# Other places for the third modulation and for the recurrence's steps in a hybrid HGRN2 and attention layer

## The reference

```python
shift_m, scale_m, gate_m, shift_f, scale_f, gate_f = ada_mod(c, w_ada, b_ada)     # silu(c) @ w_ada + b_ada
h = rms_norm(x, gain) * (1 + scale_m) + shift_m
hq, hf, hi, hg, fq, fk, fv, ff = split(h @ w_in)
# recurrence, in blocks of rows: b = cumsum(logf(hf)); k = (1 - lb) * sigmoid(-hf); v = hi
o = (q * exp(b)) @ S + att(q, k, decay of b) @ v
S = exp(b_last) * S + (k * exp(b_last - b)).T @ v
# attention: logf = log_sigmoid(ff + bias); c = cumsum(logf); softmax(q k / 8 + c_q - c_k) v
```

## Time and profile before

| what | us |
|---|---|
| median of 3 runs (773.26 to 776.86) | 774.0 |
| the profiled execution | 773.54 |
| its span, first to last instruction | 771.8 |
| PE busy | 672.2 |
| DVE busy | 381.8 |
| ACT busy | 210.1 |
| POOL busy | 216.3 |

### The profile page before, as it was taken

How to read it: one execution, slowest core, us unless ns; L and a number is a source line. 1 busy time by engine, 2 the same in 40 slices (tenths; PEclk the granted TensorE clock), 3 DMA queues, 4 the chain that set the end, 5 groups by cost and what they waited for, 6 DMA issues and landing times. The chain is left out here.

```text
span 771.8 us, 19078 instructions
## 1 busy us (share of the span) xinstructions
PE 672.2 (87%) x7455; PEld 442.2 (57%) x7455; DVE 381.8 (49%) x1053; ACT 210.1 (27%) x425; POOL 216.3 (28%) x336
## 2 busy tenths in 40 slices
PE   2999999999987969998899992699999999999920
PEld 1686476444443858665764552566666666676710
DVE  3300024200189788666645438455555555555556
ACT  4310137000161132266401110123232222232203
POOL 1212100100397620120100000234444444444440
PEclk9999999999998879999899996699999999999975
DMA  8973082536303110490095129699999999999624
GB/s 334 400 270 109 1 327 89 240 113 256 128 2 113 71 32 2 147 380 21 8 408 230 54 82 368 266 417 414 414 416 416 414 411 411 406 410 410 238 69 183
DMA packets 38417, 182.95 MB, mean 237 GB/s; under 512 B 5912, under 2 KB 6312, under 8 KB 22672
## 3 DMA queue, kind: packets, MB, share of 16 engines
q1 hardware_dynamic: 29968, 158.88, 52.0%
q0 software_dynamic: 8384, 23.12, 8.4%
HBM read 169.57 MB, written 15.28 MB: 240 GB/s over the span
## 5 line engine op out<-in xcount | busy, mean ns | idle before, releaser
L1757 PE MATMUL bank<-weights,x_hT 128*128 128x512 f32 x256 | 113.3, 601 | 0.0
L1741 PE MATMUL bank<-x_hT,weights 128*128 128x272 f32 x384 | 92.5, 403 | 0.0
L2046 PE MATMUL bank<-weights,R 128*32 128x256 f32 x1408 | 80.6, 379 | 5.1 <-issue 4.0
L1741 PEld LDWEIGHTS bank<-x_hT,weights 128*128 128x128 f32 x384 | 74.2, 195 | 16.9 <-issue 0.8
L1757 PEld LDWEIGHTS bank<-weights,x_hT 128*128 128x128 f32 x256 | 48.7, 192 | 60.4 <-issue 60.2
L845 POOL DMA_INDIRECT y_d<-R,x_hT x44 | 50.9, 1156 | 98.0 <-DVE R L1609 46.6
L2046 PEld LDWEIGHTS bank<-weights,R 128*32 128x32 f32 x1408 | 54.2, 110 | 28.5 <-issue 7.3
L1087 ACT ACT_TABLE_LOAD x44 | 56.5, 1283 | 21.0 <-DVEq L1190 20.3
L839 POOL DMA_INDIRECT R<-h_d,x_hT x46 | 48.0, 1044 | 45.8 <-POOL x_hT L858 25.4
L1087 ACT ACTIVATE R<-bank 128x128 f32<-128x128 f32 x44 | 12.2, 278 | 175.9 <-PE bank L2046 175.9
L1975 PE MATMUL bank<-weights,x_hT 128*128 128x512 f32 x128 | 58.3, 608 | 0.0
(11 more groups left out here) (346 smaller groups left out, 994.5 us busy)
## 6 DMA issues: line engine op xcount, KB each, us to landing
weights<-in_w_ada SPq DMA_DIRECT2D x24, 1024.0 KB, 11.1
weights<-in_w_exp_gate SPq DMA_DIRECT2D x16, 1024.0 KB, 10.6
weights<-in_w_exp_down SPq DMA_DIRECT2D x16, 1024.0 KB, 11.3
weights<-in_w_exp_up SPq DMA_DIRECT2D x16, 1024.0 KB, 11.3
R<-in_w_exp_down SPq DMA_DIRECT2D x16, 1024.0 KB, 11.1
weights<-in_w_in SPq DMA_DIRECT2D x7, 2048.0 KB, 8.6
R<-in_w_exp_up SPq DMA_DIRECT2D x8, 1024.0 KB, 10.9
R<-in_w_exp_gate SPq DMA_DIRECT2D x8, 1024.0 KB, 10.9
```

The lines of the kernel that those rows point to most:

```text
L1741: ins = T.matmul(bank[b][:, 0:HALF], w[:, k, h * P:(h + 1) * P], hT[:, k, c * HALF:(c + 1) * HALF], start=(n == 0), stop=(n == KT - 1))
L1757: ins = T.matmul(bank[b][:, :], hT[:, k, i * P:(i + 1) * P], w[:, k, :], start=(k == 0), stop=(k == KT - 1))
L2046: ins = T.matmul(bank[2][32 * j:32 * j + 32, 0:2 * P].rearrange("p (w f) -> p w f", w=2), XT[:, k, :], W2[:, :, k, j * P:(j + 1) * P], sta ...
```

## The change

Four things change, and all of them are order or place; no arithmetic is added or taken away.

1. The modulation's products come earlier: the first half of ada1 ahead of hg, its second half ahead of hf, ada2's halves between hf's heads and ahead of hi. The ring of loads follows. DVE reads ada1 ahead of hf's work and ada2 ahead of hi's copies; POOL stores ada2's rows ahead of all exponents.
2. Tiles of fk, their turns and the gate's logits (ff) move into `schedule`, and the recurrence's steps begin right behind hi: step -1 stands ahead of fk, and the others are spread among fk, ff, fv and fq. lfT stands behind two tiles of fv.
3. fk uses banks 6 and 7 instead of 4 and 5, its turns bank 3 instead of 6.
4. DVE prepares tile 0 of the recurrence between the third and the fourth copy of hi. POOL's stores of fk go between the exponents of tiles 2, 3 and 4, its stores of fv behind them all.

```diff
             grp(f"hg{i}", 2 + i % 2, "act")
+        grp("ada1", 1, "dve")
         for h in range(HGH):
             grp(f"hf{h}0", 4 + 2 * (h % 2), "dve")
             grp(f"hf{h}1", 5 + 2 * (h % 2), "dve")
-        grp("ada1", 1, "dve")
+        grp("ada2", 0, "dve")
         for i in range(NTILE):
             grp(f"hi{i}", 2 + i % 2, "dve")
...
-        schedule = [("fv", i) for i in range(NTILE)] + [("fq", h, c) for h in range(4) for c in range(2)]
-        for step, after in reversed(list(zip(range(-1, NTILE), (1, 4, 6, 8, 10, 11)))):
-            schedule.insert(after + 1, ("hgrn", step))
-        schedule.insert(1, ("lfT",))
+        schedule = [("hgrn", -1), ("fk", 0), ("fk", 1), ("fkT", 0), ("hgrn", 0), ("fk", 2), ("fkT", 1), ("ff",), ("fk", 3), ("fkT", 2),
+                    ("hgrn", 1), ("fk", 4), ("fv", 0), ("fv", 1), ("lfT",), ("fkT", 3), ("fkT", 4), ("hgrn", 2),
+                    ("fv", 2), ("fv", 3), ("fv", 4), ("fq", 0, 0), ("hgrn", 3),
+                    ("fq", 0, 1), ("fq", 1, 0), ("fq", 1, 1), ("fq", 2, 0), ("hgrn", 4), ("fq", 2, 1), ("fq", 3, 0), ("fq", 3, 1)]
...
+            elif item[0] == "fk":
+                grp(f"fk{item[1]}", 6 + item[1] % 2, "act")
+            elif item[0] == "fkT":
+                grp(f"fkT{item[1]}", 3, "dve")
...
-        ring += [("hf", 6, 2), ("hi", 4, 2)] + [(f"ada1_{k}", k - 4, 1) for k in range(4, 8)]
-        ring += [("fk", 6, 2)] + [(f"ada2_{k}", k, 1) for k in range(4)]
-        ring += [("fv", 4, 2)] + [(f"ada2_{k}", k - 4, 1) for k in range(4, 8)]
-        ring += [("fq", 6, 2)]
+        ring += [("hf", 6, 2)] + [(f"ada1_{k}", k - 4, 1) for k in range(4, 8)]
+        ring += [("hi", 4, 2)] + [(f"ada2_{k}", k % 4, 1) for k in range(8)]
+        ring += [("fk", 6, 2), ("fv", 4, 2), ("fq", 6, 2)]
...
-        for r, first in enumerate(("hT00", "hf00", "fk0")):
+        for r, first in enumerate(("hT00", "hg0", "hf20")):
```

On POOL:

```diff
+            mod_rows(2)
...
             exponents(0)
             exponents(1)
             pool.dma_start(S_sample, a["state_hgrn"].rearrange("l b h k v -> k (l b h) v")).then_inc(s_S0, 16)
+            filled(pool, "Db0")
+            exponents(2)
+            store_k(0)
+            store_k(1)
+            filled(pool, "Db1")
+            exponents(3)
+            store_k(2)
+            store_k(3)
+            filled(pool, "Db2")
+            exponents(4)
             taken(pool, "lfT")
...
+            store_k(4)
...
+            filled(pool, "fkT4")
...
+            for i in range(NTILE):
+                store_v(i)
```

On ACT:

```diff
             exp_levels(0)
             exp_ends(0)
             exp_levels(1)
             for item in schedule:
+                if item[0] == "fk":
+                    evict_k(item[1])
+                if item[0] == "ff":
+                    taken(act, "ff1")
+                    alink(act, A.activation(ssel[0:8, 0:TOK], cf[0:8, 0:TOK], ACT.Abs))
```

On DVE:

```diff
+            for i in range(3):
+                evict_v(i)
             dve.wait_ge(s_qs, HGH)
             end_exponents(0)
             operands(0)
             end_operands(0)
+            for i in range(3, NTILE):
+                evict_v(i)
...
             for item in schedule:
+                if item[0] == "fkT":
...
+                if item[0] == "ff":
+                    fox_sums()
```

On PE:

```diff
             feature_major("hq")
+            ada(1, 1, 0, 4)
             loaded(pe, "hg")
             for i in range(NTILE):
                 token_major("hg", i, 2 + i % 2)
-            ada(1, 1, 0, 4)
-            feature_major("hf")
             ada(1, 1, 4, KT)
+            feature_major("hf", range(2))
+            ada(2, 0, 0, 4)
+            feature_major("hf", range(2, 4))
+            ada(2, 0, 4, KT)
             loaded(pe, "hi")
             for i in range(NTILE):
                 token_major("hi", i, 2 + i % 2)
-            ada(2, 0, 0, 4)
-            loaded(pe, "fk")
...
```

More of the change, by code:

```diff
@@ L219, in build @@
                 grp("lfT", 3, "dve")
+            elif item[0] == "ff":
+                grp("ff0", 0, "dve")
+                grp("ff1", 1, "dve")
+                grp("lpT", 2, "dve")
+            elif item[0] == "fk":
+                grp(f"fk{item[1]}", 6 + item[1] % 2, "act")
+            elif item[0] == "fkT":
+                grp(f"fkT{item[1]}", 3, "dve")
             elif item[0] == "fv":
@@ L722, in _, with store_k, store_v @@
             bias_rows(2)
-            for i in range(NTILE):
+            mod_rows(2)
+            def store_k(i):
                 taken(pool, f"fk{i}")
                 pool.dma_start(kout[i * P:(i + 1) * P, :] if i < 4 else kous, fkt[i % 2][0:ROWS[i], :]).then_inc(s_kout[i % 2], 16)
-            mod_rows(2)
+            def store_v(i):
+                taken(pool, f"fv{i}")
+                pool.dma_start(vout[i * P:(i + 1) * P, :] if i < 4 else vous, v_fox[0:ROWS[i], i, :]).then_inc(s_vout, 16)
             def exponents(i):
@@ L737, in exponents @@
                     g.tensor_tensor(Xv[:, :, :, H:], bv[:, :, :, H:], anc, ALU.subtract).then_inc(s_lv, 1)
-            taken(pool, "hi0")
             exponents(0)
@@ L750, in _ @@
             pool.dma_start(cks_d, cf[0:8, SEQ:SEQ + PAST + NDEC]).then_inc(s_ckw, 16)
-            filled(pool, "Db0")
-            exponents(2)
+            store_k(4)
             pool.wait_ge(s_ckw, 32)
@@ L769, in _ @@
             pool.dma_start(fgain, bcast(a["fox_out_gain"][0], P)).then_inc(s_ckr, 16)
-            filled(pool, "Db2")
-            exponents(4)
             def mask_future(q):
@@ L948, in _, with evict_k @@
                 A.activation(kk[:, h, :], fr, ACT.Exp).then_inc(s_kk, 1)
-            for i in range(NTILE):
+            def evict_k(i):
                 n = ROWS[i]
@@ L954, in _ @@
                     filled(act, f"fkT{i - 2}")
-                b = bank[4 + i % 2]
+                b = bank[6 + i % 2]
                 if i < 4:
@@ L977, in exp_ends @@
                 A.activation(kE[i % 2][:, :, 0:n], kE[i % 2][:, :, 0:n], ACT.Exp).then_inc(s_le, 1)
[L980 to L983, removed]
             exp_levels(0)
@@ L987, in _ @@
             for item in schedule:
+                if item[0] == "fk":
[3 more added lines that the diff above has]
+                    alink(act, A.activation(ssel[0:8, 0:TOK], cf[0:8, 0:TOK], ACT.Abs))
+                    alink(act, A.activation(ssel[0:8, 0:TOK], ssel[0:8, 0:TOK], ACT.Exp, scale=-1.0))
+                    A.activation(ssel[0:8, 0:TOK], ssel[0:8, 0:TOK], ACT.Ln, bias=1.0).then_inc(s_ln, 1)
                 if item[0] == "fq":
@@ L1268, in _ @@
             filled(dve, "hT41")
+            dve.wait_ge(s_badd, 64)
+            filled(dve, "modT")
+            filled(dve, "ada1")
+            read("dve", "ada1", V.tensor_tensor(msb, bank[1][:, :], badd, ALU.add))
             for h in range(HGH):
@@ L1283, in _, with evict_v @@
                 vlink(dve, ins)
[L1284 to L1288, removed]
+            dve.wait_ge(s_badd, 96)
+            dve.wait_ge(s_modw, 32)
+            filled(dve, "ada2")
+            read("dve", "ada2", V.tensor_tensor(msb, bank[0][:, :], badd, ALU.add))
+            def evict_v(i):
                 filled(dve, f"hi{i}")
@@ L1296, in _ @@
                     read("dve", f"hi{i}", ins)
[L1297 to L1304, removed]
             known = {"le": 0}
@@ L1330, in end_operands @@
                 V.tensor_tensor(kE[i % 2][:, :, 0:n], kE[i % 2][:, :, 0:n], kk[:, :, t0:t0 + n], ALU.mult).then_inc(s_qk, 1)
[L1333 to L1344, removed]
@@ L1345, in _, with fox_sums @@
-            V.tensor_scalar(cf[0:8, :], cf[0:8, :], -float(FD) ** 0.5, None, ALU.mult).then_inc(s_cf, 1)
+            def fox_sums():
+                for c in range(2):
+                    filled(dve, f"ff{c}")
+                    read("dve", f"ff{c}", V.tensor_scalar(cf[0:8, c * HALF:(c + 1) * HALF], bank[c][0:8, 0:HALF], fbias[0:8, 0:1], None, ALU.add))
+                filled(dve, "lpT")
+                read("dve", "lpT", V.tensor_copy(lf[0:8, SEQ:SEQ + PAST], bank[2][0:8, 0:PAST]))
+                dve.wait_ge(s_ln, HGH + 1)
+                taken(dve, "ff1")
+                vlink(dve, V.scalar_tensor_tensor(lf[0:8, 0:SEQ], cf[0:8, 0:SEQ], 0.0, ssel[0:8, 0:SEQ], ALU.min, ALU.subtract))
+                V.scalar_tensor_tensor(lf[0:8, SEQ + PAST:], cf[0:8, SEQ:TOK], 0.0, ssel[0:8, SEQ:TOK], ALU.min, ALU.subtract).then_inc(s_lf, 1)
+                dve.wait_ge(s_lf, 1)
+                vlink(dve, V.tensor_tensor_scan(cf[0:8, 0:SEQ], lf[0:8, 0:SEQ], lf[0:8, 0:SEQ], 0.0, ALU.add, ALU.bypass))
+                vlink(dve, V.tensor_tensor_scan(cf[0:8, SEQ:], lf[0:8, SEQ:SEQ + 288], lf[0:8, SEQ:SEQ + 288], 0.0, ALU.add, ALU.bypass))
+                V.tensor_scalar(cf[0:8, :], cf[0:8, :], -float(FD) ** 0.5, None, ALU.mult).then_inc(s_cf, 1)
@@ L1398, in _ @@
             for item in schedule:
+                if item[0] == "fkT":
+                    i = item[1]
+                    n = ROWS[i]
```

(37 more changed lines are left out.)

9 lines of the change are left out of this document (removed).

## The result

The changed kernel takes 778.0 us, median of 20 executions, against 774.9 for 20 of the kernel before: a ratio of 1.0038, with a 95% interval of 1.0020 to 1.0055. The forecast was 766.9, and 776 was the upper end of its range. The profiled execution took 778.6 with a span of 776.8, 5.0 more than the span before; the medians differ by 3.2. A ratio leaves out executions over 1.5% above the fastest of the same kernel: two in all, both of the kernel before with POOL's exponents held back.

The account below looks back on a forecast made before the run. PE's own work, plus what DVE's recurrence makes it lose, bounds the stage. fv0 at 236.6 plus 81.5 gives 318.1 against 325.2, 7.1 less: 773.5 becomes 766.4, plus 0.5 is 766.9 us; range 762 to 776.

Parts of the forecast that it names:

- the long wait for DVE of the earlier trace: PE's 5.0 us wait for DVE ahead of fv's fifth tile in the old kernel, after which that tile took 3.64.
- attention(0), 4.9 undisturbed: 176.0: On DVE behind hi's copies: attention of tile 0 takes 4.9 us, running from 171.1 to 176.0.
- PE has fk1 at 186.4: On PE behind hi: fk1 is complete at 186.4 us, so fkT0 finds no wait for fk0's copy at 186.2.
- the moved loads I cost at nothing: On SP, up to hi: the earlier weight loads add no time; only ada2's second half was called tight, 2 us if late.
- the clock's rival: Fewer PE products from fkT3 to step 3 lower the clock; with the old 2.0 gap 5.7 us, 772.6 us, chance 0.22.
- the 15.3 us of old waits: Eight PE waits of the old kernel in the stretch of projections and recurrence, which the new 11.2 us wait was to replace.
- the bound from hi2 to fk4: DVE's work from hi2's copy to end_exponents(3) ahead of fk4's copy, one chain from 161.0 to 235.5 us, sets the pace.
- The accepted wait: PE waits 11.2 us at fv0 for fk4's bank, because on ACT exp_ends(3) stands ahead of fk4's copy.
- the last rival: The wait at fv0 is absent, only if ACT reached fk4 ahead of exp_ends(3), which its order forbids; no chance given.
- that rival's 776.3: POOL's exponents keep DVE out in operands(1) and operands(2), 9.4 us, fq ending at 327.5: 776.3 us, chance 0.16.
- DVE keeping the port: DVE holds the shared port against POOL and the clock holds: 761.8 us, chance 0.15.
- The 769.1 for three steps at 7.8: By the skill's rule all three operands steps, operands(0) too, cost 7.8 us on DVE; end 2.2 later, 769.1 us.

Follow-up runs that it names:

- two late-load runs: Changed kernel, fv's load issued only behind fk0: 773.05 us, ratio 0.9970; kernel before, fq's load issued only behind fv1: 779.4 us, ratio 1.0057.

## Why the prediction was wrong, step by step

- *Right:* hi began at 140.2 (forecast 139.6); operands(1) and (2) took 8.1 each (7.8); the wait at fv0 is there, 11.6 (11.2), with the clock down behind it; from fv0 to the attention 82.8 us passed (81.5); the long wait for DVE of the earlier trace rows is gone. No load of ada2 was late.
- *The step that failed* is "attention(0), 4.9 undisturbed: 176.0", with "PE has fk1 at 186.4" and "the moved loads I cost at nothing". Between hi's end at 169.0 and 186.4, fk0 and fk1 take 13.8, which leaves 3.6 for PE's step -1; the old kernel took 5.7 for it, 2.0 of them the row in PE's own issue. That row had no place in the chain. It stood in the clock's rival, and it is counted into "the 15.3 us of old waits" that the new wait was to replace. It falls into attention(0)'s last products, and fv's load, which SP is now free to issue just then, makes it 5.3: step -1 took PE 9.3, and attention(0) took DVE 10.2. The two late-load runs show both halves: 5.3 to 2.1 with the load taken away, 2.0 to 5.4 with one put there.
- *The sum, corrected.* Up to fk1 PE's path counts: the end of hi 0.8 late, step -1 5.7 longer, 5.3 of it the gap, and fk0 and fk1 2.1 longer at the lower clock, together 8.6. From there DVE's chain counts: attention(1) 2.6 longer, 1.4 of it the wait for the second gap and 1.2 the copies beside POOL, and all that follows up to fv0 1.4 shorter than forecast (41.6 instead of 43.0). So fv0 began at 246.4 instead of 236.6, 9.8 late. Behind fv0 another 1.3, 0.9 of it on fv0 and fv1. So the attention starts at 329.2 and not at 318.1, 11.1 later; 7.1 forecast as gain less 11.1 is the 4.0 lost.
- *DVE as "the bound from hi2 to fk4"* was half right. From attention(1) on its chain sets fv0. Before that PE's path does: over attention(0) DVE waited 4.2 for PE, and making operands(1) 3.4 shorter moved nothing. Nor did POOL stand still beside end_exponents(0), whose subtraction took 2.15 instead of 0.67, off the path.
- *The accepted wait.* "What it replaces is the 15.3 us of old waits" took 11.2 us as the price of the order. It was the price of one place in ACT's program, which the last rival named as fixed ("which its order forbids"); with fk4's copy ahead of step 1's ends the same order of steps ran 14 us shorter (ratio 0.9859 against 1.0038).
- *The parts.* The forecast never priced the moved modulation and the spread steps apart. Without the spread steps the change gave 1.1%, and the spread steps as written cost 1.5% (1.0038 over 0.9891).
- *Rivals.* POOL did not keep DVE out: no product of operands(1) or (2) took over 0.95 us, so that rival's 776.3 is the nearest time by luck. The clock's rival had the gap in it, at 2.0, and put its clock losses behind the small products from fkT3 to step 3; they came behind the two long waits. DVE keeping the port did not occur. The 769.1 for three steps at 7.8 was not tested: POOL was done with its exponents at 163.3, 0.5 us before operands(0), which took 4.7.

## What to carry to other kernels

A row "waits for its own issue" is a term of the sum like any wait, and its size is not fixed (2.0 and 5.3 us here): note at which instruction it falls and which transfers the new order will run there. When a wait is accepted because an engine's program has a slower item ahead of the one wanted, price the swap of the two first. Where a change has two parts, time them apart: here one part's gain hid behind the other's loss.

## What the runs showed of the hardware

**The gap of PE's instructions.** It came at the same product of attention(0) in every kernel with the new order, and took 1.8 to 2.5 us with quiet queues (six kernels of either order) and 4.7 to 5.4 beside 2 MB of load (five). A second gap, in attention(1), took 1.8 to 3.0 in the seven kernels with the new order. The Trainium skill, page "Runtime: NRT & Kernel Launch", section "🔬 Instruction fetch mechanics", says that instructions come in blocks of 16 KiB over a DMA queue of the sequencer's own and that crossing a block is "mostly hidden". By that rule the gap would be near nothing. The packets' size and queue agree; that the crossing is hidden does not hold for these small products. That the packet causes the gap is read from its time in eleven kernels and from the two late-load runs; the block's end was not moved on purpose.

**DVE beside POOL.** In most meetings the two alternated, at 0.83 us a product on DVE instead of 0.41. In some, all with the list and the modulation of before, one engine was kept out for about 7 us: a DVE product, a POOL subtraction, and the four copies at 7.16 above. What decides between the two is not shown. In the changed kernel POOL had begun its exponents 1.5 us before DVE's four copies, which took 2.09:

```profile
179.18 0.60 POOL L741 TENSOR_TENSOR weights<-R 128x256 f32<-128x256 f32 x1 [15.08 <-PE bank L1847]
```

In the kernel before with POOL's exponents held back it had begun 1.9 us before them, and they took 7.16. On small instructions alternating cost more in proportion than on large ones: copies of 32 partitions went from 0.91 to 2.07 a group, arithmetic on 128x4 from 0.17 to 0.55. The Trainium skill, page "SBUF — State Buffer", section "Who interferes with whom", has the exclusive hold per instruction; that fits the alternation, not the 7 us.
